# Retention in a two-block layer kernel: the value projections of all heads made ahead, with positions on the partitions, and turns of four weight blocks

## The reference, cut to what matters

```python
h = rmsnorm(x, norm_g[1])                    # 512 x 1024
proj = h @ ret_w_in[0]
q, k, v, q_mem, z = split_cols(proj, [qk_w, qk_w, MAIN_W, MEM_W, INNER])
main = retention(q, k, v)                    # 12 heads, keys of 64, values of 128
...
qf, kf = rotary(q), rotary(k) * 64 ** -0.5   # then, per head and chunk of 128 positions,
inner = (qc @ kc.T) * d_inner                # decay by distance, causal
o = inner @ vc + (qc @ R) * xi ; R = g_chunk * R + (kc * zeta).T @ vc
out = out * rsqrt(mean(out * out) + EPS)     # per head
o = concatenate([main, memo]) * silu(z) ; x = x + o @ w_out[1]
```

## Time and profile before

| | |
|---|---|
| median of 3 runs | 1894.52 us |
| the profiled execution | 1897.74 us |
| its span (what all positions below refer to) | 1896.0 us |
| TensorE matmul busy | 1863.8 us (98%) |
| VectorE / ScalarE / GpSimd busy | 844.9 / 726.5 / 768.8 us |
| mean granted clock of TensorE | 0.994 of full speed |
| retention turns, by TensorE's products | 534.20 to 788.08 us |

### The profile page before, as it was taken

The page is one execution under the profiler, slowest core; times in us unless marked ns, Lnnn a source line. Parts: engine busy times, 40 slices in busy tenths (PEclk is TensorE's granted clock), DMA queues, the critical chain, the costliest instruction groups (busy, mean ns, idle before and its releaser), DMA issues.

```text
span 1896.0 us, 24574 instructions
## 1 busy us (share of the span) xinstructions
PE 1863.8 (98%) x8540; PEld 1514.7 (80%) x8540; DVE 844.9 (45%) x1504; ACT 726.5 (38%) x1147; POOL 768.8 (41%) x362
## 2 busy tenths in 40 slices
PE   8999999999999999999999999998999989999998
PEld 6877777888877777888888888867788768888887
DVE  5332333243133344343259989936333364445202
ACT  5332333333244444333342243337233364444323
POOL 3444334444443333344444443323344454444442
PEclk9999999999999999999999999999999999999999
DMA  6323333333332323333333433312233323333322
GB/s 184 90 75 86 88 87 85 88 96 89 99 104 85 89 78 88 89 100 89 98 91 100 96 95 90 79 36 71 78 98 96 100 78 89 93 95 100 111 91 99
DMA packets 311967, 174.00 MB, mean 92 GB/s; under 512 B 16369, under 2 KB 304649, under 8 KB 311905
## 3 DMA queue, kind: packets, MB, share of 16 engines
q1 hardware_dynamic: 298960, 165.17, 30.4%
q0 software_dynamic: 2448, 7.93, 1.6%
q10 hardware_dynamic: 10496, 0.07, 0.3%
HBM read 170.95 MB, written 2.20 MB: 91 GB/s over the span
## 4 chain that ended last, share of the span: by engine, by line
PE 93%; DVE 2%; DMA 2%; ACT 2%; issue 1%; POOL 0%; SPq 0%; DVEq 0%; ACTq 0%; POOLq 0%
PE proj L1775 24%; PE proj L1777 24%; PE proj L1776 24%; PE PV L1909 1%; PE A L1877 1%; PE A L2276 1%; PE A L2278 1%; PE A L2277 1%; DVE A L1458 1%; PE PV L1913 1%; PE A L1883 1%; PE A L1964 1%; PE PV L1964 1%; DMA wraw<-w_in 1%; PE A L1893 1%; PE A L1971 1%
## 5 line engine op out<-in xcount | busy, mean ns | idle before, releaser
L495 POOL TENSOR_TENSOR wlo<-wraw,whi 128x1024 fp32r<-128x1024 f32 (+1 forms) x305 | 723.5, 2375 | 1075.6 <-ACT whi L604 1075.6
L1775 PE MATMUL proj<-Hh,whi 128*128 128x512 f32 x1640 | 659.8, 402 | 0.4 <-DVE uv L1711 0.2
L1777 PE MATMUL proj<-Hh,wlo 128*128 128x512 f32 x1640 | 640.5, 391 | 0.0
L1776 PE MATMUL proj<-Hl,whi 128*128 128x512 f32 x1640 | 639.6, 390 | 0.0
L604 ACT ACTIVATE whi<-wraw 128x1024 fp32r<-128x1024 f32 (+1 forms) x304 | 318.6, 1048 | 769.1 <-DMA wraw<-fox_w_in 176.1
L1775 PEld LDWEIGHTS proj<-Hh,whi 128*128 128x128 f32 x1640 | 308.9, 188 | 70.3 <-issue 7.4
L1776 PEld LDWEIGHTS proj<-Hl,whi 128*128 128x128 f32 x1640 | 308.9, 188 | 68.3 <-issue 6.9
L1777 PEld LDWEIGHTS proj<-Hh,wlo 128*128 128x128 f32 x1640 | 308.4, 188 | 65.6
L1458 DVE SCALAR_TENSOR_TENSOR A<-cin,dwT,A 128x512 f32<-128x512 f32 x232 | 175.1, 755 | 6.8
L1775 PE MATMUL proj<-Oh,whi 128*128 128x512 f32 x256 | 101.0, 394 | 0.0
L1777 PE MATMUL proj<-Oh,wlo 128*128 128x512 f32 x256 | 99.7, 389 | 0.0
(11 more groups left out here) (408 smaller groups left out, 2461.2 us busy)
## 6 DMA issues: line engine op xcount, KB each, us to landing
wraw<-w_in SPq DMA_DIRECT2D x68, 512.0 KB, 3.8
wraw<-fox_w_in SPq DMA_DIRECT2D x57, 512.0 KB, 3.9
wraw<-ret_w_in SPq DMA_DIRECT2D x44, 512.0 KB, 3.8
wraw<-w_up SPq DMA_DIRECT2D x44, 512.0 KB, 3.8
wraw<-w_out SPq DMA_DIRECT2D x40, 512.0 KB, 4.0
wraw<-w_down SPq DMA_DIRECT2D x22, 512.0 KB, 3.4
wraw<-w_mem_kv SPq DMA_DIRECT2D x16, 512.0 KB, 4.0
wraw<-conv_pw_w SPq DMA_DIRECT2D x8, 512.0 KB, 4.0
```

The lines of the kernel that those rows point to most:

```text
L495: pool.tensor_tensor(wlo[s][:, 0:r, :], wraw[s][:, 0:r, :], whi[s][:, 0:r, :].bitcast(F32), ALU.subtract).then_inc(w_lo, 1)
L1775: mm(dst, whi[s][:, c, :], xh, start=(first and c == 0), stop=False)
L1776: mm(dst, whi[s][:, c, :], xl, start=False, stop=False)
L1777: ins = mm(dst, wlo[s][:, c, :], xh, start=False, stop=(last and c == chunks - 1))
```

## The change

- A new phase `val1` of 12 weight blocks stands ahead of the retention turns. Each block is 256 rows by 512 columns of the value weights (four heads); four blocks make the values of four heads. `values_of` uses slices of `Hh`, `Hl` as the loaded operand and the weights as the moving one, so that the result has positions on the partitions: 2 chunks x 4 tiles of 128 positions x 3 = 24 matmuls of 128x512 a block, into four PSUM banks, with another set of four for the next group of heads.
- ScalarE copies each finished bank into `values` (`keep_values`), scaled by the norm's root, which now has to lie on the partitions: four matmuls of one column turn `rms` into four columns, and one small VectorE operation scales them. `values` lies where `Oh` of the 12 heads comes later; `ret_values` reads it.
- Turns have four blocks (query, key, z, z). The transposes, the evictions to `vT` and the copies to `vtok` go. Turns are written out on TensorE, ScalarE and VectorE; SP and GpSimd keep a loop.
- The order moves: the scores follow block 2, block 3 follows them, the values end the turn. Squares, the last tanh and the roots stand at the start of the next turn on ScalarE (`ret_finish`), and the two means stand after two chunks of the next turn's block 0 on TensorE. VectorE rotates the query ahead of the gate and outputs of the turn before, and the key behind them.

The diff, cut to its core (left out: names of semaphores and of the columns `v_roots = small[:, 84:88]`, the table of turns, and the same index change in `ret_tanh` and `softmax_turn`):

```diff
@@ -82,7 +82,7 @@
         ("forget", 1, 1, 1), ("fox", HEADS, 4, 4), ("mem0", MEM_HEADS, 4, 4), ("wo0", KC // 2, 4, 2),
-        ("ret", HEADS // 2, 6, 6), ("mem1", MEM_HEADS, 4, 4), ("wo1", KC // 2, 4, 2),
+        ("val1", 1, HEADS, 0), ("ret", HEADS // 2, 4, 4), ("mem1", MEM_HEADS, 4, 4), ("wo1", KC // 2, 4, 2),
@@ -153,6 +153,8 @@
         with ExitStack() as one:
+            with ExitStack() as kept:
+                values = sb("values", [P, HEADS, S], F32, kept)
...
@@ -357,8 +361,9 @@
             if name == "ret":
-                col = i * P + b * HEADS * DK if b < 2 else i * (2 * P) + [V_RET, V_RET + P, Z_RET, Z_RET + P][b - 2]
-                return w_ret, col, 0, 8
+                return w_ret, i * P + b * HEADS * DK if b < 2 else i * (2 * P) + Z_RET + (b - 2) * P, 0, 8
+            if name == "val1":
+                return w_ret, V_RET + b // 4 * S, b % 4 * 2, 8
...
@@ -406,6 +411,15 @@
         ret_sum = (PV, A[0])
+        v_banks = (A, (*proj, PV, VT), A)
+
+        def by_columns(x):
+
+            return x[:].rearrange("p c n -> p (c n)").rearrange("p (c n) -> p c n", c=2)
+
+        def kept_values(group, j):
+
+            return values[:, 4 * group:4 * group + 4, j * P:(j + 1) * P]
@@ -420,6 +434,8 @@
                     sp.dma_start(wraw[s][:].rearrange("p c n -> p (c n)"), w[row * P:(row + 1) * P, :]).then_inc(w_landed[s], 16)
+                elif name == "val1":
+                    sp.dma_start(by_columns(wraw[s]), w[:, row:row + 2, col:col + S]).then_inc(w_landed[s], 16)
@@ -527,13 +543,13 @@
 
-            def ret_turn(i, par):
+            def ret_turn(i):
                 for e in range(2):
                     since(pool, r_decayed, 2 * i + (e - 1))
                     src = t["c_decay"][2 * i + e] if isinstance(i, int) else t["c_decay"][bass.ds(2 * i + e, 1)].rearrange("a p n -> (a p) n")
                     pool.dma_start(decay[e][:], src).then_inc(in_decay[e], 16)
-                for b in range(6):
-                    split("ret", i, b, par)
+                for b in range(4):
+                    split("ret", i, b)
@@ -547,12 +563,12 @@
             turns("wo0")
+            for b in range(HEADS):
+                split("val1", 0, b)
             pool.wait_ge(maxed, HEADS)
-            ret_turn(0, 0)
-            ret_turn(1, 1)
-            with pool.Fori(1, HEADS // 4) as h:
-                for par in range(2):
-                    ret_turn(h * 2 + par, par)
+            ret_turn(0)
+            with pool.Fori(1, HEADS // 2) as i:
+                ret_turn(i)
@@ -703,9 +719,7 @@
                 if before == "ret":
-                    ret_tanh(HEADS // 2 - 1, 1)
-                    ret_rms(HEADS - 2, 0)
-                    ret_rms(HEADS - 1, 1)
+                    ret_finish(HEADS // 2 - 1)
...
@@ -751,34 +765,36 @@
 
-            def ret_vtok(r, e):
-                act.wait_ge(r_vturned, r + 1)
-                f(vtok[e][:].rearrange("p a b -> p (a b)"), VT[:], ACT.Copy).then_inc(r_v, 1)
-
-            def ret_turn(i, before, par):
-                if before:
-                    ret_tanh(i - 1, 1)
-                    ret_rms(i * 2 - 2, 0)
-                    ret_rms(i * 2 - 1, 1)
-                split("ret", i, 0, par)
+            def keep_values(group):
+
+                for j in range(NT):
+                    if j < NT - 1:
+                        act.wait_ge(v_summed, (NT - 1) * group + j + 1)
+                    else:
+                        act.wait_ge(w_used, PH["val1"].n(0, 4 * group + 3) + 1)
+                    f(kept_values(group, j), v_banks[group][j][:].rearrange("p (h n) -> p h n", h=4), ACT.Identity,
+                      scale=v_roots[:, j:j + 1]).then_inc(v_kept, 1)
+
+            def ret_finish(i):
+
+                ret_square(i * 2, 0)
+                ret_square(i * 2 + 1, 1)
+                ret_tanh(i, 1)
+                ret_rms(i * 2, 0)
+                ret_rms(i * 2 + 1, 1)
+
+            def ret_turn(i):
+                if i:
+                    ret_finish(i - 1)
+                split("ret", i, 0)
                 since(act, r_roped, i * 2)
-                if not before:
-                    act.wait_ge(rms_ready, 2)
-                else:
-                    act.wait_ge(r_v, i * 2)
                 ret_swap(i, 0)
-                split("ret", i, 1, par)
+                split("ret", i, 1)
                 act.wait_ge(r_roped, i * 2 + 1)
                 ret_swap(i, 1)
-                split("ret", i, 2, par)
-                split("ret", i, 3, par)
-                ret_vtok(i * 2, 0)
-                ret_vtok(i * 2 + 1, 1)
-                split("ret", i, 4, par)
+                split("ret", i, 2)
                 ret_tanh(i, 0)
-                ret_square(i * 2, 0)
-                ret_square(i * 2 + 1, 1)
-                split("ret", i, 5, par)
+                split("ret", i, 3)
@@ -834,13 +850,16 @@
             rms_of(VT, rms, 1)
-            ret_turn(0, False, 0)
-            ret_turn(1, True, 1)
-            with act.Fori(1, HEADS // 4) as h:
-                own.turns(1, HEADS // 4, 4, h)
-                for par in range(2):
-                    ret_turn(h * 2 + par, True, par)
-            own.after()
+            for b in range(HEADS):
+                if b == 4:
+                    act.wait_ge(v_rooted, 1)
+                if b in (4, 8):
+                    keep_values(b // 4 - 1)
+                split("val1", 0, b)
+            keep_values(2)
+            act.wait_ge(v_kept, 8)
+            for i in range(HEADS // 2):
+                ret_turn(i)
@@ -1330,28 +1349,23 @@
 
-            def ret_turn(i, before):
+            def ret_turn(i):
                 ph = PH["ret"]
-                if before:
+                rope(i, 0, q)
+                if i:
                     ret_gate(i - 1, 1)
                     ret_out(i * 2 - 2, 0)
                     ret_out(i * 2 - 1, 1)
-                rope(i, 0, q)
                 rope(i, 1, k)
                 arrived("ret", i, 2)
-                tt(vT[:], proj[ph.bank(2)][:], rms[:], ALU.mult).then_inc(evac, 1)
-                arrived("ret", i, 3)
-                dve.wait_ge(r_vturned, i * 2 + 1)
-                tt(vT[:], proj[ph.bank(3)][:], rms[:], ALU.mult).then_inc(evac, 1)
+                since(dve, r_table, i * 2 - 1)
+                tt(z[0][:], proj[ph.bank(2)][:], rms[:], ALU.mult).then_inc(evac, 1)
+                ret_gate(i, 0)
                 ret_decay(i * 2, 0, i)
                 ret_decay(i * 2 + 1, 1, i)
-                arrived("ret", i, 4)
-                since(dve, r_table, i * 2 - 1)
-                tt(z[0][:], proj[ph.bank(4)][:], rms[:], ALU.mult).then_inc(evac, 1)
-                ret_gate(i, 0)
-                arrived("ret", i, 5)
+                arrived("ret", i, 3)
                 since(dve, r_table, i * 2)
-                tt(z[1][:], proj[ph.bank(5)][:], rms[:], ALU.mult).then_inc(evac, 1)
+                tt(z[1][:], proj[ph.bank(3)][:], rms[:], ALU.mult).then_inc(evac, 1)
@@ -1411,13 +1425,10 @@
             own.settle()
-            ret_turn(0, False)
-            ret_turn(1, True)
-            with dve.Fori(1, HEADS // 4) as h:
-                own.turns(1, HEADS // 4, 16, h)
-                for par in range(2):
-                    ret_turn(h * 2 + par, True)
-            own.after()
+            dve.wait_ge(v_spread, 1)
+            ts(v_roots, VT[:, 0:NT], float(D // P), None, ALU.mult).then_inc(v_rooted, 1)
+            for i in range(HEADS // 2):
+                ret_turn(i)
@@ -1929,7 +1940,7 @@
                 if before:
-                    products(name, i, 0, 0, H)
+                    products(name, i, 0, 0, H, each=ret_means(HEADS // 2 - 1) if before == "ret" else None)
@@ -1959,9 +1970,8 @@
                 pe.wait_ge(r_decayed, r + 2 - e)
-                pe.wait_ge(r_v, r + 1)
                 for j in range(NT):
-                    ins = mm(ret_sum[e][:, j * P:S], vtok[e][:, j, :], decayed[e][:, TRI[j]:TRI[j] + S - j * P],
+                    ins = mm(ret_sum[e][:, j * P:S], values[:, r, j * P:(j + 1) * P], decayed[e][:, TRI[j]:TRI[j] + S - j * P],
@@ -1970,34 +1980,37 @@
 
-            def ret_turn_values(i, e):
-                pe.wait_ge(evac, PH["ret"].g(i, 2 + e) + 1)
-                if e == 0:
-                    pe.wait_ge(r_roped, i * 2 + 2)
-                since(pe, r_v, i * 2 + e)
-                for j in range(NT):
-                    ins = pe.transpose(VT[:, j * P:(j + 1) * P], vT[:, j * P:(j + 1) * P], ident[:])
-                ins.then_inc(r_vturned, 1)
-
-            def ret_turn(i, before, par):
-                if before:
-                    products("ret", i, 0, 0, H, par=par)
-                else:
-
-                    products("ret", i, 0, 0, H, par=par, each=lambda c: pe.wait_ge(h_ready, KC + c + 1))
-                    statistics(KC)
-                products("ret", i, 1, 1, H, par=par)
-                products("ret", i, 2, 2, H, par=par)
```

(65 more changed lines are left out.)

## The result

The changed kernel is slower, by 0.3%. Its median was 1900.24 us (1898.4 to 1903.76, ten executions) against 1895.26 for the kernel before (ten); the ratio is 1.0031, 95% interval 1.0020 to 1.0042. 1904.1 was predicted, range 1895 to 1912. Over all 23 the median is 1901.6.

The account below looks back on a forecast made before the run. TensorE was taken to bound the kernel, busy throughout the retention stage. Terms -5.6 (transposes), +1.1 (roots), -0.3 (query wait), +11.0 (stall) and +3.4 (clock) gave +9.6 us, 1904.1 us, range 1895 to 1912.

Parts of the forecast that it names:

- The transposes' 5.6 us: TensorE, retention turns: transposes ahead of and behind the scores go, 0.94 us a turn, 5.6 us gained in six.
- the value blocks: TensorE, ahead of the turns: twelve blocks of 24 products only swap operand roles, at no cost.
- The roots: TensorE, between value blocks 1 and 2: four added matmuls put roots onto partitions, 1.1 us (0.4 to 1.8).
- The wait for the query in turn 0: TensorE, turn 0: the wait for the rotated query goes, 0.3 us gained.
- The stall: TensorE at the scores, turns 1 to 5: waits 2.2 us each for the rotated key, 11.0 us (10.0 to 13.0).
- the two outputs: VectorE, between gate and key rotation: two outputs of the turn before take 5.79 us of the key's chain.
- Turn 0 and what comes next: Retention turns: turn 0 has no outputs to make, so no stall; decay, squares, means and weights cause no wait.
- The clock: TensorE behind the new gaps: half speed for 3.4 us loses 1.7 us, charged at two of five gaps.
- stall without the clock: Rival, chance 0.26: TensorE stalls at the scores but keeps its clock; +6.2 us, 1900.7 us.
- the forecast: Likeliest case, chance 0.39: stall at the scores, clock lost at some gaps; 1904.1 us, 1902.4 to 1905.8 with one to three.
- the charge of 3.4 us: TensorE clock term: half speed behind two of the five gaps costs 3.4 us; bounds 0 to 8.5.
- The collision of gate and split: VectorE's gate against GpSimd's split: should just miss; otherwise up to 1.05 us, 5.3 in five. Rival shared with clock losses, 0.18.

Follow-up runs that it names:

- the doubled groups: The kernel before with every group of four value transposes issued twice; the stage took 265.06 us, 5.28 more for twelve groups.
- the kernel with the outputs first: The changed kernel with VectorE's gate and both outputs of the turn before put ahead of the query's rotation; 1889.01 us, on another chip 1891.05 us.
- the first series: The changed kernel unaltered, its first ten executions against the kernel before; median 1900.24 us, ratio 1.0031.
- the other two: The changed kernel unaltered, measured two more times; 1907.11 us (seven executions, ratio 1.0051) and 1904.91 us (six, ratio 1.0044).

## Why the prediction was right, and where it was off

- **Where the work went**: right. The transposes' 5.6 us were 5.3 by the doubled groups; the value blocks came at no cost in their new form and TensorE never waited for a bank, a weight or a copy. The roots cost 1.0 us (0.81, and 0.18 in the 13 blocks behind them, which took 70.90 us where 13 of 5.44 make 70.72), 1.1 was taken. The wait for the query in turn 0 was worth 0.25 us (three blocks behind the statistics took 540.09 to 557.11, 17.02 us; 16.32 and the 0.45 that the first product behind the statistics costs make 16.77) and is gone, 0.3 was taken. The three make -4.6, -4.8 was forecast, and the kernel with the outputs first measured -4.46.
- **The stall**: right in place, number and cause; five of them at the scores, for the key. Its size was 2.2 each by the prediction and 1.97 in the stage (9.84 for five), under the lower bound of 2.0 by a hair. The mis-sized term is the two outputs: 579.86 to 585.65 holds 0.2 us that belong to the start of the next operation in that turn; written out, two outputs take 704.81 to 710.37, 5.56. The prediction had named that bound and taken the other side.
- **Turn 0 and what comes next**: nothing else became late. Decays, squares, means and loads fitted, as worked out. The turns took 32.4 us (680.12 to 712.48), predicted 32.5.
- **The clock**: the mechanism was right, and two of five was near the mean but above it: 0, 1 and 3 in three profiles, 1.3. A charge worked out from one gap of 2.05 us and one of 1.38 could not tell that; that it came near is in part luck. A loss costs 1.6 us where 1.7 was said. By their clocks and times the executions of the first series lost none or few, which is the rival "stall without the clock" (1900.7 predicted, 1900.24 measured); those of the other two hold many that lost several, which is the forecast (1904.1 predicted, 1907.1 and 1904.9 measured). So the step that failed in the first series is the charge of 3.4 us. In its profile the stage lost 5.4 us where 9.6 were forecast for the change: 3.4 of the difference is this charge, 1.2 the five stalls, and 0.3 the other way the rest. Beside the kernel before in the same series the medians stood 5.0, 10.4 and 9.6 us higher, so how near +9.6 looks depends on the series. Why the share differs between series stays open; nothing in the program differs.
- **The collision of gate and split**: it missed, by little. The gate ran 704.21 to 704.89 and GpSimd's split began at 704.92. In the kernel with the outputs first another gate (677.78) took 1.01 us instead of 0.69 beside a split that ran to 678.23, and nobody waited for it. The Trainium skill ("SBUF — State Buffer", SBUF: two separate sides) has a VectorE operation with two SBUF inputs and a GpSimd operation that reads SBUF exclude each other; the longer gate agrees. No run here made them collide in this chain, so its price there is not shown.

## What to carry to other kernels

When the engine that bounds a kernel is never idle, shortening its work also shortens the cover of everybody else: count, for each result that it will wait for, the operations between its release and its need, in the order in which the other engine's queue holds them. Here one block less of cover and an output moved behind the query turned a gain of 4.5 us into a loss of 5, and swapping two lines gave it back (1889 to 1891 us, ratio 0.996 to 0.998, faster than both kernels). Price overlapped matmuls by the distance between starts, and measure a changed stage by marks inside it, since the profiles here differ by up to 7 us outside of it (1630 to 1638 us).

## What was not expected of the hardware

A TensorE gap of 1.82 us can be followed by 3.4 us at 1.2 GHz or by none, in the same kernel at the same place, from one execution to the next. Over the eight profiles with gaps none of five gaps of 1.2 us was followed by it, 2 of 13 of 1.8, 2 of 3 of 2.2, 3 of 4 of 2.3, 4 of 5 of 2.4, and all ten of 3.0 and 4.7. The gap that the prediction took its charge from (2.05 us at 1326.38) does the same. It stands in all 14 profiles of this record at 2.0 to 2.1 us, and the clock fell behind it in ten. The two profiles of the kernel with the outputs first differ in it; behind a gap of 2.06 us that ended at 1317.79 in the first and at 1319.76 in the second:

```profile
1318.30:1321.60 3.30, 3.30 (x9) 2.53 (x9) 2.21 (x1) 0.00 (x0) 1.66 (x1) 0.50 0.00 0
...
1320.00:1324.00 4.00, 4.00 (x19) 3.27 (x19) 2.50 (x1) 0.00 (x0) 1.95 (x1) 1.00 0.00 0
```

Nor is a gap of 3 us always followed by a fall: one in front of other work (it ended at 1230.04 and 1232.32, 3.04 and 3.05 us) was in the first of the two and not in the second. What decides it is not shown.

A stall near 2 us therefore has a price of two parts: its own length, and 1.6 us times a chance. It also adds to the spread of a kernel's times: 12 us between the fastest and the slowest of 23 executions here, 4.4 for 17 of the version without the gaps, 8.5 for 57 of the kernel before.
